# Nine MLP rounds: the second product as seven products of half size instead of eight

## The reference, cut to what matters

```
x = x + jnp.square(jax.nn.relu(h2 @ w_ff1)) @ w_ff2     # h2: 512 x 1024, w_ff1: 1024 x 4096, w_ff2: 4096 x 1024
```

## Time and profile before

| | |
|---|---|
| median of three runs | 2013.65 us |
| the profiled execution | 2011.3 us, its span 2009.5 us |
| TensorE busy | 1989.0 us (99%) |
| VectorE busy | 1050.4 us (52%) |
| ScalarE busy | 732.2 us (36%) |
| mean granted TensorE clock | 0.999 of 2.4 GHz |
| DMA | 188.27 MB, mean 94 GB/s |

### The profile page before, as it was taken

The page is one execution under the profiler, slowest core; times in us unless marked ns, Lnnn a source line. Parts: engine busy times, 40 slices in busy tenths (PEclk is TensorE's granted clock), DMA queues, the critical chain, the costliest instruction groups (busy, mean ns, idle before and its releaser), DMA issues.

```text
span 2009.5 us, 23416 instructions
## 1 busy us (share of the span) xinstructions
PE 1989.0 (99%) x10007; PEld 1684.6 (84%) x10007; DVE 1050.4 (52%) x982; ACT 732.2 (36%) x786; POOL 133.3 (7%) x188
## 2 busy tenths in 40 slices
PE   9999999999999999999999999999999999999998
PEld 8788888888988888898888888888898888888886
DVE  7466586655533342477777733333454464343335
ACT  5464553352423131345555423132342234132222
POOL 0100151000100000030000100000010010000000
PEclk9999999999999999999999999999999999999999
DMA  5222112123332323332222332232323233323221
GB/s 192 91 74 74 63 64 84 63 106 115 106 100 89 105 86 102 105 103 69 69 69 84 106 105 96 93 104 85 104 85 104 90 107 114 103 86 104 89 100 63
DMA packets 99094, 188.27 MB, mean 94 GB/s; under 512 B 4398, under 2 KB 16832, under 8 KB 99008
## 3 DMA queue, kind: packets, MB, share of 16 engines
q1 hardware_dynamic: 94704, 176.17, 26.5%
q0 software_dynamic: 4016, 10.77, 1.9%
q10 hardware_dynamic: 288, 0.07, 0.0%
HBM read 183.85 MB, written 2.10 MB: 93 GB/s over the span
## 4 chain that ended last, share of the span: by engine, by line
PE 90%; DVE 5%; ACT 2%; POOL 1%; DMA 1%; issue 1%; DVEq 0%; POOLq 0%; ACTq 0%
PE ps L797 51%; PE ps L1025 10%; PE ps L809 5%; PE ps L761 5%; PE ps L834 4%; PE ps L1276 2%; PE ps L1270 2%; PE ps L1223 1%; PE ps L868 1%; PE ps L1129 1%; PE ps L1295 1%; PE ps L1081 1%; PE ps L1053 1%; PE ps L1419 1%; DVE w_lo L1987 1%
## 5 line engine op out<-in xcount | busy, mean ns | idle before, releaser
L1987 DVE TENSOR_TENSOR w_lo<-w_raw,w_hi 128x2048 fp32r<-128x2048 f32 x126 | 288.8, 2292 | 667.0 <-ACT w_hi L1477 666.8
L1477 ACT ACTIVATE w_hi<-w_raw 128x2048 fp32r<-128x2048 f32 x126 | 241.5, 1917 | 787.3 <-PE ps L797 663.2
L797 PE MATMUL ps<-a_hi,w_hi 128*128 128x512 f32 x880 | 342.5, 389 | 0.8 <-DVE qk L2809 0.8
L797 PE MATMUL ps<-a_lo,w_hi 128*128 128x512 f32 x880 | 342.4, 389 | 0.0
L797 PE MATMUL ps<-a_hi,w_lo 128*128 128x512 f32 x880 | 342.3, 389 | 0.0
L797 PE MATMUL ps<-w_hi,h_hi 128*128 128x512 f32 x592 | 230.3, 389 | 0.0
L797 PE MATMUL ps<-w_lo,h_hi 128*128 128x512 f32 x592 | 230.3, 389 | 0.0
L797 PE MATMUL ps<-w_hi,h_lo 128*128 128x512 f32 x592 | 230.3, 389 | 0.0
L797 PEld LDWEIGHTS ps<-a_hi,w_hi 128*128 128x128 f32 x880 | 165.2, 188 | 35.4 <-issue 1.2
L797 PEld LDWEIGHTS ps<-a_lo,w_hi 128*128 128x128 f32 x880 | 165.2, 188 | 34.2
L797 PEld LDWEIGHTS ps<-a_hi,w_lo 128*128 128x128 f32 x880 | 165.2, 188 | 34.2
(11 more groups left out here) (405 smaller groups left out, 3303.1 us busy)
## 6 DMA issues: line engine op xcount, KB each, us to landing
w_raw<-in_w_ff SPq DMA_DIRECT2D x32, 1024.0 KB, 5.2
w_raw<-in_mlp_w_up SPq DMA_DIRECT2D x32, 1024.0 KB, 5.4
w_raw<-in_mlp_w_down SPq DMA_DIRECT2D x32, 1024.0 KB, 5.1
w_raw<-in_w_in SPq DMA_DIRECT2D x24, 1024.0 KB, 5.1
w_raw<-in_attn_w_qkv SPq DMA_DIRECT2D x12, 1024.0 KB, 5.1
w_raw<-in_conv_w_in SPq DMA_DIRECT2D x12, 1024.0 KB, 5.1
w_raw<-in_w_proj_gla SPq DMA_DIRECT2D x4, 1024.0 KB, 5.0
w_raw<-in_w_out SPq DMA_DIRECT2D x4, 1024.0 KB, 5.1
```

Of the source, the lines that this page charges most:

```text
L797: last = mm(ps[:, bank0 + j], left, right, start=(k == 0 and x == 0), stop=(k == QUAD * quads - 1 and x == 2), skip_group_check=halves)
L1477: nc.scalar.activation(w_hi[:, s], w_raw[:, s], ACT.Copy).then_inc(hi_ready, 1)
L1987: tt(w_lo[:, s], w_raw[:, s], w_hi[:, s].bitcast(F32), ALU.subtract).then_inc(lo_ready, 1)
```

## The change

In rounds 0 to 2 of each MLP the second product is a product of two 2 x 2 block matrices, the hidden part with quarters of 256 tokens by 512 features (11, 12, 21, 22) and the round's weights with quarters of 512 by 512. Strassen's scheme (a variant of it) makes it with seven products of quarters instead of eight. Each of the seven (`product`) is a quad of its own, of 4 (k) x 2 (token tiles) x 3 = 24 matmuls. The order of the queue is `ITEMS`: p1, p7, p2, p6, p5, p4, p3, then the four quads u0 to u3 of the next round's first product.

- Four of the seven need a sum of weight quarters (`weight_sum`, VectorE, 2048 elements each); these lie in the raw slots A and B and in new raw buffers C to F. p1 and p7 are loaded into A and B when u2 and u3 are split; p3 and p2 into C and D.
- The hidden part is kept in float32 by quarters. Relu and square are both ScalarE's now, in place; the operands' sums are VectorE's, their high parts ScalarE's (`operand`), their low parts VectorE's (`operand_lo`).
- u1 and u3 are made tile by tile with a mark after the second tile (`half_made`), except for u1 of round 0.
- Products p6, p4 and p3 are accumulated onto p1's, p7's and p2's or p5's banks. VectorE adds the banks into `acc` in eight steps (`y_add` of 1024 elements, `lower_adds` with 1024 elements from PSUM into 2048 of `acc` by a broadcast). In round 0 of the second and third MLP the first adds are copies, and the clearing of `y_tm` ahead of them is gone.
- Loops of rounds are written out; some semaphores of single steps are replaced by the engine's own step counter.

The diff, cut to its core (eight leading blanks left out):

```
+FAST = ROUNDS - 1
+ITEMS = ("p1", "p7", "p2", "p6", "p5", "p4", "p3", "u0", "u1", "u2", "u3")
...
+raw_at = [w_raw[:, 0], w_raw[:, 1]] + [z_.rearrange("p (a n) -> p a n", a=QUAD)
+                                       for z_ in (arena[:, 0:2048], arena[:, 2048:4096], tmp, qkf[:, 4096:6144])]
+h_raw = [qkf[:, 2048 * u:2048 * (u + 1)].rearrange("p (half a n) -> p half a n", half=2, a=4) for u in range(2)]
+quarter = {"11": qkf[:, 0:1024], "21": qkf[:, 1024:2048], "12": qkf[:, 2048:3072], "22": qkf[:, 3072:4096]}
+op_hi = [hhf[:, 1024 * k:1024 * (k + 1)] for k in range(4)]
+op_lo = [hlf[:, 1024 * k:1024 * (k + 1)] for k in range(4)]
...
+    def load_raw(n, src):
+        if raw_free[n]:
+            sp.wait_ge(lo_ready, raw_free[n])
+        sp.dma_start(raw_at[raw_slot[n]], src.rearrange("(a p) n -> p a n", p=P)).then_inc(raw_full[raw_slot[n]], 16)
...
+        up_part(0, 0)
+        up_part(0, 1)
+        for r in range(FAST):
+            up_part(r, 2)
+            if r == 0:
+                up_part(r, 3)
+                sp.wait_ge(quad_done, ph[name].q)
+            load_raw(item(name, r, "p3"), part(down, r * D + NBLK, NBLK))
+            load_raw(item(name, r, "p2"), part(down, r * D + NBLK, 0))
+            if r:
+                up_part(r, 3)
+            load_raw(item(name, r, "p1"), part(down, r * D, 0))
+            load_raw(item(name, r, "p7"), part(down, r * D, NBLK))
+            up_part(r + 1, 0)
+            up_part(r + 1, 1)
...
+    def product(n, op, bank, start):
+        s = n % 2
+        hi, lo = (z_[op].rearrange("p (a n) -> p a n", a=QUAD) for z_ in (op_hi, op_lo))
+        for i in range(2):
+            is_ = slice(P * i, P * (i + 1))
+            for a in range(QUAD):
+                for x, (left, right) in enumerate(((hi, w_hi), (hi, w_lo), (lo, w_hi))):
+                    last = mm(ps[:, bank + i], left[:, a, is_], right[:, s, a], start=(start and a == 0 and x == 0),
+                              stop=True, skip_group_check=True)
+        last.then_inc(quad_done, 1)
...
+    def fast_round(name, r, chunks):
+        p = ph[name]
+        b0, b1 = 4 * (p.b % 2), 4 * ((p.b + 1) % 2)
+        added = ADDS * (FAST * MLPS.index(name) + r)
+        chunk, squares_ = chunks + PRODUCTS * r, exps_at(name, r)
+        operands = {"p1": (0, b0, 1), "p7": (1, b0 + 2, 2), "p2": (2, b1, 3), "p6": (3, b0, 4),
+                    "p4": (0, b0 + 2, 5), "p5": (1, b1 + 2, 6), "p3": (2, b1 + 2, 7)}
+        for which in ITEMS:
+            if which[0] == "u":
+                up_quad(name, r + 1, int(which[1]))
+                continue
+            op, bank, number = operands[which]
+            n = item(name, r, which)
+            if which == "p1":
+                pe.wait_ge(exp_ready, squares_ + 2)
+            if which == "p2":
+                pe.wait_ge(exp_ready, squares_ + 4)
+            if which == "p6":
+                pe.wait_ge(y_added, added + 1)
+            if which == "p4":
+                pe.wait_ge(y_added, added + 2)
+            if which == "p3":
+                pe.wait_ge(y_added, added + 6)
+            pe.wait_ge(lo_ready, n + 1)
+            pe.wait_ge(chunk_lo, chunk + number)
+            product(n, op, bank, which not in ("p6", "p4", "p3"))
...
+    def split_quad(n):
+        if n in sums_at:
+            act.wait_ge(w_summed, sums_at[n])
+        else:
+            act.wait_ge(raw_full[raw_slot[n]], 16 * raw_fill[n])
+        act.wait_ge(quad_done, n - 1)
+        nc.scalar.activation(w_hi[:, n % 2], raw_at[raw_slot[n]], ACT.Copy).then_inc(hi_ready, 1)
...
+    def relu(name, r, u, c):
+        bank = 4 * ((ph[name].b + u) % 2) + 2 * c
+        if c == 0 and (r or u):
+            act.wait_ge(half_made, half_number(name, r, u))
+        else:
+            act.wait_ge(quad_done, item(name, r, f"u{2 * u + 1}") + 1)
+        dst = h_raw[u][:, :, 2 * c:2 * c + 2]
+        src = ps[:, bank:bank + 2].rearrange("p a (half n) -> p half a n", half=2)
+        step(nc.scalar.activation(dst, src, ACT.Relu))
+        nc.scalar.activation(dst, dst, ACT.Square).then_inc(exp_ready, 1)
+    def operand(src, op, ready=None, used=None):
+        if ready is not None:
+            act.wait_ge(*ready)
+        if used is not None:
+            act.wait_ge(quad_done, used + 1)
+        nc.scalar.activation(op_hi[op], quarter[src], ACT.Copy).then_inc(chunk_hi, 1)
+    def fast_round(name, r, f32):
+        sq, f = exps_at(name, r), f32 + 4 * r
+        def weights(which):
+            split_quad(item(name, r, which))
+        weights("u2")
+        relu(name, r, 0, 0)
+        relu(name, r, 0, 1)
+        operand("11", 0, (exp_ready, sq + 2))
+        weights("u3")
+        operand("11", 1, (chunk_f32, f + 1))
+        weights("p1")
+        relu(name, r, 1, 0)
+        weights("p7")
+        relu(name, r, 1, 1)
+        operand("12", 2, (exp_ready, sq + 4))
+        weights("p2")
+        operand("11", 3, (chunk_f32, f + 2))
+        operand("22", 0, None, item(name, r, "p1"))
+        weights("p6")
+        operand("21", 1, (chunk_f32, f + 3), item(name, r, "p7"))
+        weights("p5")
+        operand("12", 2, (chunk_f32, f + 4), item(name, r, "p2"))
+        weights("p4")
+        weights("p3")
+        split_quad(item(name, r + 1, "u0"))
+        split_quad(item(name, r + 1, "u1"))
...
+    def fast_round(name, r, chunks, f32, acc):
         p = ph[name]
...
+        b0, b1 = 4 * (p.b % 2), 4 * ((p.b + 1) % 2)
+        sq, f, chunk = exps_at(name, r), f32 + 4 * r, chunks + PRODUCTS * r
+        added = ADDS * (FAST * MLPS.index(name) + r)
+        fresh = r == 0 and name != "mlp0"
+        def weights(which):
+            split_quad(item(name, r, which))
+        def y_add(number, which, bank, rows, half, first=False):
+            dve.wait_ge(quad_done, item(name, r, which) + 1)
+            dve.wait_ge(y_added, added + number - 1)
+            d = acc[:, 2 * rows:2 * rows + 2, NBLK * half:NBLK * (half + 1)]
+            if first and fresh:
+                return nc.vector.tensor_copy(d, ps[:, bank:bank + 2])
+            return tt(d, ps[:, bank:bank + 2], d, ALU.add)
+        def lower_adds():
+            dve.wait_ge(y_added, added + 4)
+            d = acc[:, 2:4, :].rearrange("p i (half n) -> p i half n", half=2)
+            v = ps[:, b0:b0 + 2].rearrange("p i (one n) -> p i one n", one=1)
+            if fresh:
+                nc.vector.tensor_copy(d[:, :, 0], ps[:, b0:b0 + 2])
+                tt(d[:, :, 1], ps[:, b0:b0 + 2], d[:, :, 1], ALU.add).then_inc(y_added, 1)
+            else:
+                tt(d, v.to_broadcast([P, 2, 2, NBLK]), d, ALU.add).then_inc(y_added, 1)
+        def operand_lo(number, src, op):
+            dve.wait_ge(chunk_hi, chunk + number)
+            tt(op_lo[op], quarter[src], op_hi[op].bitcast(F32), ALU.subtract).then_inc(chunk_lo, 1)
+        def weight_sum(which, dst, x, y, loads):
+            for w_ in loads:
+                n = item(name, r, w_)
+                dve.wait_ge(raw_full[raw_slot[n]], 16 * raw_fill[n])
+            tt(raw_at[dst], raw_at[x], raw_at[y], ALU.subtract).then_inc(w_summed, 1)
+        weights("u2")
+        operand_lo(1, "11", 0)
+        dve.wait_ge(chunk_lo, chunk + 1)
+        tt(quarter["11"], quarter["11"], quarter["21"], ALU.subtract).then_inc(chunk_f32, 1)
+        weights("u3")
+        operand_lo(2, "11", 1)
+        weight_sum("p5", F_RAW, B_RAW, A_RAW, ("p1", "p7"))
+        dve.wait_ge(w_summed, sum_number(name, r, "p5"))
+        weight_sum("p7", B_RAW, C_RAW, B_RAW, ("p3",))
+        weights("p1")
+        dve.wait_ge(lo_ready, item(name, r, "p1") + 1)
+        weight_sum("p6", A_RAW, C_RAW, F_RAW, ())
+        dve.wait_ge(w_summed, sum_number(name, r, "p6"))
+        weight_sum("p4", E_RAW, D_RAW, A_RAW, ("p2",))
+        weights("p7")
+        dve.wait_ge(exp_ready, sq + 4)
+        dve.wait_ge(chunk_lo, chunk + 2)
+        tt(quarter["11"], quarter["22"], quarter["11"], ALU.subtract).then_inc(chunk_f32, 1)
+        operand_lo(3, "12", 2)
+        y_add(1, "p1", b0, 0, 0, True).then_inc(y_added, 1)
+        weights("p2")
+        operand_lo(4, "11", 3)
+        dve.wait_ge(chunk_f32, f + 2)
+        tt(quarter["21"], quarter["21"], quarter["22"], ALU.add).then_inc(chunk_f32, 1)
+        weights("p6")
+        y_add(2, "p7", b0 + 2, 1, 1, True).then_inc(y_added, 1)
+        operand_lo(5, "22", 0)
+        y_add(3, "p2", b1, 0, 0).then_inc(y_added, 1)
+        weights("p5")
+        operand_lo(6, "21", 1)
+        y_add(4, "p6", b0, 0, 1, True).then_inc(y_added, 1)
+        lower_adds()
+        dve.wait_ge(chunk_lo, chunk + 4)
+        tt(quarter["12"], quarter["12"], quarter["11"], ALU.subtract).then_inc(chunk_f32, 1)
+        weights("p4")
+        y_add(6, "p5", b1 + 2, 1, 1).then_inc(y_added, 1)
+        operand_lo(7, "12", 2)
+        weights("p3")
+        y_add(7, "p4", b0 + 2, 1, 0).then_inc(y_added, 1)
+        split_quad(item(name, r + 1, "u0"))
```

(67 more changed lines are left out.)

308 lines of the change are left out of this document (133 added, 175 removed).

## The result

The changed kernel takes 2034.82 us, the median of four runs (2030.69 to 2039.16), against 2013.95 us of the kernel before (now the median of four): a ratio of 1.0107 (1.0076 to 1.0137). It is slower by 1.1%, where 2018.5 us had been forecast; the time lies 4 us above the range's upper end. The profiled execution took 2039.16 us, with a span of 2037.4.

What follows compares the result with a forecast made beforehand. TensorE's number of matmuls was taken to bound the rounds; six steady rounds (-0.8), three first ones (+5.5) and 0.1 made +4.8 us on 2011.3, or 2016.1, and 2018.5 us on the runs' median footing, range 2011 to 2031.

Steps and rivals of the forecast that it cites:

- the saving: Second product of each changed round: 24 matmuls fewer, 5.44 us a round, 49.0 us in nine if TensorE never waits.
- the queues: VectorE and ScalarE: only 5.44 us for a product, queues strictly in written order, so the order doesn't fit.
- The named knot: At p4: its split queues behind ScalarE's copy of quarter 12, which waits on VectorE's adds and difference; 4.46 us lost.
- The timetable: One round's instructions followed on VectorE, ScalarE and TensorE: 5.31 us lost in a steady round, 7.27 in a first one.
- The restart: TensorE after a real wait: first matmul 0.14 us after VectorE's end, second 0.10 later than usual, 0.24 us in all.
- rival 3: Lower add on VectorE goes by its reads, 1.22 us instead of 2.28: 9.5 us less, 2009.0 us; chance 0.10.
- The sum of +4.8 us: All nine changed rounds: -0.8 for six steady, +5.5 for three first ones, +0.1 for the lower add's copies.
- the stalls as worked out and at most a few falls of the clock: Rival 1, the nine changed rounds: 2018.5 us, own range 2012 to 2025; chance 0.60.
- the clock falls 3.7 us after TensorE stops: Read from one instance at the earlier trace's end; the 4.2 us gap at p4 is a little longer.
- rival 2: Clock falls in most of the nine gaps at p4: 16.7 us more, 2035 us; half of them, 2027; chance 0.17.
- 1.85 us was the estimate: Cost of one clock fall at p4's gap: 3.7 us at half speed; lower bound nothing.
- The checks named: Profile after: TensorE 49 us less busy, nine waits of 4.3 us at p4, short ones at p7, p2, p5; rounds 86.9 us.

Runs made afterwards that it cites:

- the last arrangement: Changed kernel with sums and loads arranged otherwise, ScalarE's split of p4 before the copy of quarter 12, VectorE's queue reordered; 1961.93 us, 0.9760 of the kernel before, fastest of all.
- The filled kernel: Changed kernel with 18 matmuls of unused result issued before p4's wait in each of the nine rounds; 2016.10 us, 1.0020 of the kernel before.
- the kernel with nine filling matmuls: Changed kernel with nine matmuls of unused result right behind p5 in each of the nine rounds; 2026.56 us, 1.0081 of the kernel before.
- the arrangement of loads: Changed kernel with p7's raw weights in the slot free early, p1's in the late one, and other weight sums; 2026.44 us, 1.0069 of the kernel before.
- the kernel before held up: Kernel before, without the change, with five unused VectorE reductions ahead of its split in block 1 of each of nine rounds; 2073.89 us, ratio 1.0307.
- the later four times: The changed kernel unaltered, run again for a second trace and times; median 2031.85 us, 1.0107 of the kernel before.

## Why the prediction was wrong

**The bound, the saving, the queues: right.** TensorE's matmuls bound the rounds, 24 of them are worth 5.44 us, and the last arrangement got all nine times 5.44 back. The named knot is the one that the trace shows, link by link.

**The timetable: right, two terms a little large.** Counted from p1's start at 653.10, VectorE's split of u3 ended at -13.8 (forecast -13.68), the sums began at -8.74 (-8.27) since the weights landed 4.9 us after their issue and not 5.2, and the split of p7 ended at 4.94 (5.40). That is before p7's turn, so p7 and p2 lost nothing in such rounds, where I had 0.42. In a first round p1 and p7 waited, as forecast: p7 started 6.8 us after p1, 1.4 us late (by the timetable 0.20 + 1.96, less the 0.75 that p1 itself is late). p5 and p4 came 0.4 to 0.5 us early: p4 at 31.87 (32.41, VectorE's 32.27 and 0.14), after 4.06 us of idle time (4.2). The restart was a little cheaper than the 0.24: p4's first matmul started 0.10 us behind VectorE's end. The lower add took 2.29 us: it goes by the elements written, and rival 3 is dead. The sum of +4.8 us measures as +4.0 (2.2 to 5.8) with the clock held up, and that is partly luck. In the trace of the changed kernel a steady round without its fall is 88.82 - 2.26 = 86.56 us, 0.48 below 87.04, where 0.13 had been forecast. With the first rounds near their forecast, this makes some 2 to 3 us over the nine. The filled kernel's profiled execution was nearer to 4.8 because of late landings in its second MLP, where three such transfers stand on the chain with 6.28, 5.90 and 6.19 us; the first of them:

```profile
1149.47 6.28 DMA w_raw<-in_mlp_w_down
```

**The step that failed: the clock.** The prediction's sum has no term for the clock. It put "the stalls as worked out and at most a few falls of the clock" at 0.60, and falls in most of the nine gaps at 0.17, and its range ended at 2031, below that rival's own 2035. The runs show nine falls in nine gaps. It had the place and the idle time right, and read from the earlier trace rows that the clock falls 3.7 us after TensorE stops; 4.2 us looked only just longer. That one row was taken as a threshold. In the first round of the kernel after, the clock fell 2.4 us after TensorE stopped, in the kernel with nine filling matmuls after 2.05 us of idle time were already over. So the delay differs from one idle time to the next, and a single instance says no more than that it can be as long as 3.7. In 36 idle times of 4.0 us and more (two executions of the changed kernel, one of the arrangement of loads, one of the kernel before held up) the clock fell 36 times. The Trainium skill (TensorE: Matmul & The Clock Gate, Why this matters for your kernels) advises against idle gaps between bursts of matmuls. The prediction weighed its rule and gave it one chance in six; for idle times of 4.0 us and more these traces agree with it.

**The size of a fall.** 1.85 us was the estimate, down for as long as it took to fall. Measured on p4 and p3 it is 2.3 us (20.8 over nine) in the first execution and 2.0 (17.6 over nine) in the second; by the times, 15.8 us for nine, 1.75 each, with the late landings in the filled kernel. The account closes for both profiled executions within a microsecond or so: 2 to 3 us of waits, 20.8 of falls and 5.3 between the MLPs make 28 to 29, and the first is 27.9 above the 2011.3 before; 2 to 3 and 17.6 make about 20, and the second is 19.2 above. So rival 2's 2035 us met the measured 2034.8 partly by luck: its falls were priced below what the first execution shows, its stalls above, and the 5.3 us between the MLPs were in none of its terms.

**The checks named.** TensorE's busy time fell by 17.7 us and not by 49, mostly since the page counts a matmul at half speed for longer; I should have tied that check to the clock. In the fastest kernel, with no fall in a round, it is 1939.2 us, 49.8 less. The waits nine times at p4, the short ones at p7 and p5, ScalarE's order and the lower add showed as named; a wait of p2 didn't, and a steady round was 88.8 us, 86.56 and a fall, where 86.9 was named.

**What stays open.** Why the clock stays down for the shorter time in some falls (about 12.8 us for p4 and p3) and for the longer in others (13.4 and more) was not tried, nor why the landings differ by a microsecond between executions. The four first times of the changed kernel lie in two pairs, near 2031 and near 2039. The two profiles, 2037.4 and 2028.7, show 5.3 us of that in the transfers between the MLPs with their fall, and 2.4 in the MLPs. That the other runs split in the same way is not shown, and the later four times (2030.5, 2030.6, 2033.1, 2035.8) don't lie in two pairs.

## What to carry to other kernels

An engine that is busy for half of the time can still be the one that sets the pace, once the unit of TensorE's work gets shorter: write the queues out one against the other and ask at each handover who stands ahead of the instruction that TensorE needs, and for what that one waits. Behind a wait of TensorE that you leave in, count with a fall of the clock: here one came in 36 of 36 idle times of 4.0 us and more, in five of nine of 2 us and in none of nine of 1.1 us. Here 45.6 of the 70 us between the changed kernel and the best order went to one copy in the wrong place. The whole saving of 5.44 us a round came back by changing the order and the buffers alone, not the amount of work.

## What the runs showed of the hardware

The granted clock can fall while TensorE is busy again: after an idle time of 2.05 us it fell 0.8 us into the next burst, and with some 2 us idle there were falls in five of nine rounds. With 1.1 to 1.2 us idle there were falls in none of nine, with 4.0 and more in all 36. A fall cost about 2 us of TensorE's time (1.75 to 2.3 by the ways of measuring above), about half of what the 4.1 us wait itself costs. The low stretch isn't always of one length: in the first round it lasted 6.8 us in the first execution of the changed kernel and 3.4 in the second (by windows as above, 595.80 to 599.22). 18 matmuls a round whose result nobody wants were worth 15.8 us in nine rounds. An add on VectorE that reads 1024 elements from PSUM and writes 2048 through a broadcast took 2.29 us, as one of 2048 does.
